# Three 256-column fp32r matmuls per weight tile into one accumulation, PSUM results read by their users, and a modulation reduced into rows, in a single-core two-block transformer kernel

## The reference, cut to what matters

```python
p  = rms_norm(x, norm_mix) @ w_in                       # w_in
h  = x + concat(rwkv7_group(p), dsa_group(p)) @ w_mix_out      # mixer, mix_out
h  = h + memory_cross_attention(rms_norm(h), rms_norm(mem))    # kv, q, o
h  = h + square(relu(rms_norm(h) @ w_up)) @ w_down      # mlp
h  = rms_norm(h, norm_final)                            # norm "final"
m  = silu(c) @ ada_w + ada_b                            # modulation: 6 vectors of 2048
n  = modulate(rmsnorm(h, g0), m[0], m[1])               # norm "g0"
z  = gelu(n @ a_w_in); u, v = split(z)                  # a_v, a_uo
s  = w_s . rmsnorm(v) + b_s                             # mixing over 128 tokens
h  = h + m[2] * ((u * s) @ a_w_out)                     # a_uo
n  = modulate(rmsnorm(h, g1), m[3], m[4])               # norm "g1"
g, v = split(dwconv(n @ ffn_w_up))                      # ffn, ffn_tail
h  = h + m[5] * ((silu(g) * v) @ ffn_w_down)
out = rmsnorm(h, final_g)                               # norm "out"
```

## Time and profile before

| | |
|---|---|
| time, median of 3 runs | 3272.32 us (3270.5 to 3272.33) |
| the profiled execution, its own time | 3279.74 us |
| its span in the profile | 3277.9 us |
| granted TensorE clock, mean | 0.924 |
| PE busy | 89% |
| PEld (weight loads) busy | 77% |
| DVE busy | 68% |
| ACT busy | 43% |
| HBM read | 568.08 MB, 174 GB/s over the span |
| chain that ended last | PE 82%, DVE 12%, issue 3%, ACT 2%, DMA 1% |

### The profile page before, as it was taken

The page is one execution under the profiler, slowest core; times in us unless marked ns, Lnnn a source line. Parts: engine busy times, 40 slices in busy tenths (PEclk is TensorE's granted clock), DMA queues, the critical chain, the costliest instruction groups (busy, mean ns, idle before and its releaser), DMA issues.

```text
span 3277.9 us, 49683 instructions
## 1 busy us (share of the span) xinstructions
PE 2922.4 (89%) x16638; PEld 2516.7 (77%) x16638; DVE 2228.9 (68%) x3447; ACT 1413.6 (43%) x2225; POOL 167.1 (5%) x204
## 2 busy tenths in 40 slices
PE   7997765665898899999999799799998999999997
PEld 6886654553686688888888678788887888888886
DVE  5445666656575887878878554588786775666666
ACT  5444121212444544444444255454444554554554
POOL 0002300000210100000001101000000000000001
PEclk9999777785798899999999699999998999999999
DMA  5553000010343577787877345277774555555553
GB/s 187 190 186 104 1 6 6 6 51 4 120 163 103 193 284 272 277 284 271 284 273 267 139 149 192 102 283 284 268 273 139 189 184 187 186 188 191 177 191 135
DMA packets 157042, 572.65 MB, mean 175 GB/s; under 512 B 17440, under 2 KB 17824, under 8 KB 156480
## 3 DMA queue, kind: packets, MB, share of 16 engines
q1 hardware_dynamic: 154512, 562.37, 49.8%
q10 hardware_dynamic: 2304, 7.75, 0.7%
q0 software_dynamic: 48, 0.13, 0.0%
HBM read 568.08 MB, written 2.10 MB: 174 GB/s over the span
## 4 chain that ended last, share of the span: by engine, by line
PE 82%; DVE 12%; issue 3%; ACT 2%; DMA 1%; DVEq 0%; POOL 0%; ACTq 0%; POOLq 0%; SPq 0%
PE ps L1684 45%; PE ps L1685 24%; PE ps L1687 3%; PE ps L1750 1%; DVE wlo L1403 1%; PE ps L598 1%; PE ps L587 1%; PE ps L604 1%; DVE xx L404 1%; ACT whi L1230 1%; DVE bt L385 1%; DVE lm L381 0%; PE ps L606 0%; DVE tt L1430 0%; DVE rn L357 0%
## 5 line engine op out<-in xcount | busy, mean ns | idle before, releaser
L1684 PE MATMUL ps<-xn,whi 128*128 128x512 f32 x4080 | 1457.3, 401 | 55.5 <-DVE xn L1469 36.0
L1403 DVE TENSOR_TENSOR wlo<-raw,whi 128x1024 fp32r<-128x1024 f32 x872 | 1058.5, 1228 | 445.7 <-ACT whi L1230 436.9
L1685 PE MATMUL ps<-xn,wlo 128*128 128x256 f32 x4352 | 1216.7, 282 | 0.0
L1230 ACT ACTIVATE whi<-raw 128x1024 fp32r<-128x1024 f32 x872 | 906.2, 1054 | 611.2 <-PE ps L1685 583.9
L1684 PEld LDWEIGHTS ps<-xn,whi 128*128 128x128 f32 x4080 | 773.5, 190 | 249.2 <-issue 48.1
L1684 PE MATMUL ps<-act_in,whi 128*128 128x512 f32 x2444 | 872.5, 401 | 11.2 <-issue 3.8
L1685 PEld LDWEIGHTS ps<-xn,wlo 128*128 128x128 f32 x4352 | 829.0, 190 | 5.6
L1685 PE MATMUL ps<-act_in,wlo 128*128 128x256 f32 x2624 | 732.3, 282 | 0.0
L1684 PEld LDWEIGHTS ps<-act_in,whi 128*128 128x128 f32 x2444 | 462.7, 189 | 126.9 <-DVE wlo L1403 5.2
L1685 PEld LDWEIGHTS ps<-act_in,wlo 128*128 128x128 f32 x2624 | 498.9, 190 | 3.9
L1237 ACT ACTIVATE hl<-ps 128x256 f32<-128x256 f32 x452 | 169.0, 376 | 388.6 <-PE ps L1687 388.6
(11 more groups left out here) (317 smaller groups left out, 2372.1 us busy)
## 6 DMA issues: line engine op xcount, KB each, us to landing
raw<-in_stream SPq DMA_DIRECT2D x872, 512.0 KB, 4.2
adaw<-in_ada SPq DMA_DIRECT2D x96, 512.0 KB, 5.9
adaq<-in_ada SPq DMA_DIRECT2D x96, 512.0 KB, 4.9
h<-in_xT SPq DMA_DIRECT2D x4, 512.0 KB, 6.7
lw<-in_lora ACTq DMA_DIRECT2D x8, 256.0 KB, 2.5
memx<-in_memT ACTq DMA_DIRECT2D x1, 2048.0 KB, 8.8
out<-fin SPq DMA_DIRECT2D x4, 512.0 KB, 2.6
wst<-in_wsT ACTq DMA_DIRECT2D x1, 1024.0 KB, 5.0
```

Source lines behind the costliest of these rows:

```text
L1230: act.activation(whi[:, r, :], raw[:, r, :], ACT.Copy).then_inc(hi_done, 1)
L1403: dve.tensor_tensor(wlo[:, r, :], raw[:, r, :], whi[:, r, :].bitcast(F32), ALU.subtract)\
L1684: pe.matmul(ps[:, b, :], whi[:, r, w], x[:, kc, :], start=first, stop=False)
L1685: ins = pe.matmul(ps[:, b, 0:T], wlo[:, r, w], x[:, kc, 0:T], start=False, stop=False)
```

## The change

- **Matmuls.** A pair becomes three matmuls of 256 columns, all into columns 0:256 of the bank: `whi` with the high part, `whi` with the low part, `wlo` with the high part. The order is the same in all chunks. There are 20928 stream matmuls in place of 13952, and as many weight loads; the columns are as many as before.
- **Evacuation.** `half`, `add`, `hl` and `evac_done` go. The user of a tile reads the bank: ACT copies (w_in, kv, q), relu (mlp), gelu (a_v, a_uo), copy and middle tap (ffn); DVE the residual add to `h`. Two counters, `evac_act` and `evac_dve`, say who has emptied a bank; `bank_free` makes PE wait for the right one. The mlp's square is a `tensor_tensor` on DVE.
- **Waits of the squares.** The wait for POOL's sums moves from DVE's residual to ACT's square.
- **Initial count.** `evac_act` is raised by 8 on ACT, behind `prepare("mix")`.
- **Tail.** For q, o, mlp, a_v and a_uo the four splits ahead stand behind the last tile in place of between the last tiles, on ACT and DVE.
- **Modulation.** PE multiplies each accumulator (512 columns, moving) with a 16- or 8-column slice of a mostly zero matrix `pick`, which puts the sum of accumulator a into row a of one bank; ACT copies the rows to SBUF (`rows`); four transposes turn them (`turn_modulation`). Part of this stands ahead of `stat` (5 of 16, 4 of 8), the rest behind it.

```diff
-def schedule(loop, iters, lens, split, evac, primed=False, ahead=None, aside=None):
+def schedule(loop, iters, lens, split, evac, primed=False, ahead=None, aside=None, tail_first=False):
...
                 split(i + 1, p - S)
-            elif ahead and p - S < RING:
+            elif ahead and p - S < RING and not tail_first:
                 ahead(0, p - S)
             for g, t in due.get(p, ()):
                 evac(i, g, t)
             if aside:
                 aside(i, p)
+        if last and ahead and tail_first:
+            for p in range(RING):
+                ahead(0, p)
...
+    def evacuated(self, i, g, t):
+
+        w = self.who[g]
+        return w, self.before[w] + 4 * (i * self.who.count(w) + self.who[:g].count(w)) + t + 1
...
+    EVAC = {"A": evac_act, "D": evac_dve}
+
+    def all_evacuated(eng, nm):
+
+        for w in "AD":
+            if L[nm].before[w]:
+                eng.wait_ge(EVAC[w], L[nm].before[w])
+
+    def bank_free(eng, lin, i, g, t):
+
+        if g >= 2:
+            w, v = lin.evacuated(i, g - 2, t)
+        elif isinstance(i, int) and i == 0 and lin.g0:
+            before, k, q = last_two[lin.g0 + g - 2]
+            w, v = before.evacuated(k, q, t)
+        else:
+            w, v = lin.evacuated(i - 1, len(lin.lens) + g - 2, t)
+        eng.wait_ge(EVAC[w], v)
 
...
-        def half(lin, i, g, t):
+        def copy_out(lin, i, g, t, dst):
 
             tile_wait(act, lin, i, g, t)
-            act.wait_ge(evac_done, lin.tile(i, g, t) + 5)
-            act.activation(hl[:, t, :], ps[:, lin.bank(g, t), T:2 * T], ACT.Copy).then_inc(hl_done, 1)
+            act.activation(dst, ps[:, lin.bank(g, t), 0:T], ACT.Copy).then_inc(evac_act, 1)
...
+                    act.wait_ge(EVAC[w], v)
+                    act.wait_ge(ss_done, SQ_AT[nm] + max(0, (2 if nm == "mlp" else 1) * (j - 3)))
                     act.activation(tt[:, t, :], h[:, j, :], ACT.Square).then_inc(sq_done, 1)
...
         prepare("mix")
-        run("w_in", half)
+        act.sem_inc(evac_act, 8)
+        run("w_in", lambda lin, i, g, t: copy_out(lin, i, g, t, one(proj[:, bass.ds(8 * i + 4 * g + t, 1), 1:TW])
+                                                  if not isinstance(i, int) else proj[:, 8 * i + 4 * g + t, 1:TW]))
         mixer["scalar"](act)
...
         def mlp(lin, i, g, t):
+            def relu(t):
+                tile_wait(act, lin, i, g, t)
+                act.wait_ge(ai_ready, AI["mlp"] + 16 * i + 4 * g + t + 1)
+                act.activation(tt[:, t, :], ps[:, lin.bank(g, t), 0:T], ACT.Relu).then_inc(evac_act, 1)
             if g < 4:
-                staged(t, lambda t: half(lin, i, g, t), lambda t: high("mlp", i, 4 * g + t))
+                staged(t, relu, lambda t: high("mlp", i, 4 * g + t))
             else:
-                staged(t, lambda t: half(lin, i, g, t), residual("mlp", i, 4)(g))
+                residual("mlp", i, 4)(g)(t)
         run("mlp", mlp)
+        def rows(nm, sums, n):
+
+            act.wait_ge(ada_red, 1 if nm == "g0" else 3)
+            act.activation(sums[0:n, 0, :], ps[0:n, red_bank[nm], :], ACT.Copy).then_inc(row_done, 1)
...
                 def middle(t):
 
-                    act.wait_ge(evac_done, lin.tile(i, g, t) + 9)
+                    tile_wait(act, lin, i, g, t)
+                    act.wait_ge(y_sum, 2 * (k4 + t) + 2)
+                    z = ps[:, lin.bank(g, t), 0:T]
+                    act.activation(zc[:, t, 1:T + 1], z, ACT.Copy).then_inc(z_done, 1)
+                    act.wait_ge(r_done, AI[nm] + 16 * i + 2 * g - 1 + t % 2)
                     apart(act)
                     a = FC[nm] + 16 * i + 2 * g + t % 2
                     c = COL["conv"] + 8 * a + 4 * (t // 2)
                     w = lambda q: par[:, c + q:c + q + 1] if isinstance(c, int) else par[:, bass.ds(c + q, 1)]
-                    act.activation(yc[:, t, :], zc[:, t, 1:T + 1], ACT.Identity, bias=w(3), scale=w(1))\
-                       .then_inc(y_done, 1)
+                    act.activation(yc[:, t, :], z, ACT.Identity, bias=w(3), scale=w(1)).then_inc(evac_act, 1)
...
+                    tile_wait(dve, L[nm], i, g, t)
+                    y = ps[:, L[nm].bank(g, t), 0:T]
+                    if gate is None:
+                        ins = dve.tensor_tensor(h[:, m, :], y, h[:, m, :], ALU.add)
                     else:
-                        dve.wait_ge(ss_done, SQ_AT[nm] + max(0, m - 3))
-                    add(L[nm], i, g, t, tt[:, t, :])
-                    dve.wait_ge(evac_done, L[nm].tile(i, g, t) + 9)
-                    if gate is None:
-                        ins = dve.tensor_tensor(h[:, m, :], h[:, m, :], tt[:, t, :], ALU.add)
-                    else:
-                        ins = dve.scalar_tensor_tensor(h[:, m, :], tt[:, t, :], mod[:, gate + m:gate + m + 1],
+                        ins = dve.scalar_tensor_tensor(h[:, m, :], y, mod[:, gate + m:gate + m + 1],
                                                        h[:, m, :], ALU.mult, ALU.add)
-                    ins.then_inc(h_sum, 1)
+                    ins.then_inc(evac_dve, 1)
...
                         if first:
-                            pe.wait_ge(evac_done, lin.tile(i, g, t) + 1)
-                        b = lin.bank(g, t)
+                            bank_free(pe, lin, i, g, t)
+                        y = ps[:, lin.bank(g, t), 0:T]
                         w = slice(c * 512 + t * P, c * 512 + (t + 1) * P)
-                        if not last:
-                            pe.matmul(ps[:, b, :], whi[:, r, w], x[:, kc, :], start=first, stop=False)
-                        ins = pe.matmul(ps[:, b, 0:T], wlo[:, r, w], x[:, kc, 0:T], start=False, stop=False)
-                        if last:
-                            ins = pe.matmul(ps[:, b, :], whi[:, r, w], x[:, kc, :], start=False, stop=True)
-                            if t < 3:
-                                ins.then_inc(tile_done, 1)
+                        pe.matmul(y, whi[:, r, w], x[:, kc, 0:T], start=first, stop=False)
+                        pe.matmul(y, whi[:, r, w], x[:, kc, T:2 * T], start=False, stop=False)
+                        ins = pe.matmul(y, wlo[:, r, w], x[:, kc, 0:T], start=False, stop=last)
+                        if last and t < 3:
+                            ins.then_inc(tile_done, 1)
                 ins.then_inc(slot_used, 1)
...
+        def reduce_modulation(nm, after, sums, n, part):
+
+            b = red_bank[nm]
+            bank_free(pe, L[after], 0, 0, 1)
+            for a in part:
+                pe.wait_ge(ada_sum, 7 + 2 * ((0 if nm == "g0" else ADA_MLP) + 8 * a + 8))
+                ins = pe.matmul(ps[0:n, b, :], pick[:, 15 - a:15 - a + n], sums[:, a, :], start=a == 0, stop=a == n - 1)
+            if n - 1 in part:
+                ins.then_inc(ada_red, 1)
+
+        def turn_modulation(nm, sums, n):
+
+            pe.wait_ge(row_done, 1 if nm == "g0" else 2)
+            for t in range(4):
+                ins = pe.transpose(ps[:, red_bank[nm], t * n:(t + 1) * n], sums[0:n, 0, t * P:(t + 1) * P], ident[0:n, 0:n])
             ins.then_inc(ada_red, 1)
-        reduce_modulation("g0", L["a_v"].g0, ada, 16)
-        stat("final", L["a_v"].g0)
+        reduce_modulation("g0", "a_v", ada, 16, range(5))
+        stat("final", first_free("a_v"))
         pe.matmul(ps[:, stat_bank["final"], T:2 * T], ones[:, :], sg[:, :], start=True, stop=True).then_inc(stat_done, 1)
+        reduce_modulation("g0", "a_v", ada, 16, range(5, 16))
```

More of the change, by code:

```diff
@@ L885, in one @@
         return x.rearrange("p a c -> p (a c)")
-    L, n, g = {}, 0, 0
-    for name, it, lens in [("w_in", 6, [8, 8]), ("mix_out", 1, [8] * 4), ("kv", 1, [8, 8]), ("q", 1, [8]),
-                           ("o", 1, [2] * 4), ("mlp", 4, [8] * 8), ("a_v", 4, [8, 8]), ("a_uo", 2, [8] * 8),
-                           ("ffn", 2, [8] * 12), ("ffn_tail", 1, [8] * 6 + [6] * 4)]:
-        L[name] = Lin(n, g, lens, it)
+    L, n, g, before, last_two = {}, 0, 0, {"A": 8, "D": 0}, {}
+    for name, it, lens, who in [("w_in", 6, [8, 8], "AA"), ("mix_out", 1, [8] * 4, "DDDD"), ("kv", 1, [8, 8], "AA"),
+                                ("q", 1, [8], "A"), ("o", 1, [2] * 4, "DDDD"), ("mlp", 4, [8] * 8, "AAAADDDD"),
+                                ("a_v", 4, [8, 8], "AA"), ("a_uo", 2, [8] * 8, "AAAADDDD"),
+                                ("ffn", 2, [8] * 12, "AAAAAAAADDDD"), ("ffn_tail", 1, [8] * 6 + [6] * 4, "AAAAAADDDD")]:
+        L[name] = Lin(n, g, lens, it, who, dict(before))
         n += it * sum(lens)
         g += it * len(lens)
+        for w in "AD":
+            before[w] += 4 * it * who.count(w)
+        for q in range(len(lens)):
+            last_two[g - len(lens) + q] = (L[name], it - 1, q)
     NSLOT = n
@@ L901, in build @@
              "ffn": "ffn_tail"}
+    TAIL_FIRST = ("q", "o", "mlp", "a_v", "a_uo")
     w_landed = [sem(f"w_landed{r}") for r in range(RING)]
@@ L926, in build @@
```

(21 more changed lines are left out.)

165 lines of the change are left out of this document (79 added, 86 removed).

## The result

The changed kernel takes 3303.07 us (median of 4, 3301.97 to 3304.11) against 3272.32; ratio 1.0094, interval 1.0077 to 1.0112. Its profiled execution took 3303.39, with a span of 3301.6. I had forecast 3241 and a range up to 3266.

What follows compares the result with a forecast made beforehand. PE was taken as the bound, its 6976 pairs filling some 2460 of 3278 us. Terms summing to -30.8 took the profiled 3279.74 to 3248.9; less 7.4, that execution's excess over the median, 3241, range 3221 to 3266.

Steps and rivals of the forecast that it cites:

- The stream: PE's matmul stream: three 256-column matmuls take 0.3532 us where a pair took 0.353, +3 us (bounds -15 to +19).
- Rival 1: PE's matmul stream: a third weight load shows, 16 ns each, +112 us, 3353 us; chance 0.09.
- Rival 2: Longer loop bodies of w_in and a_v pay 1.6 to 2.9 us a turn, +15 us, 3256 us; chance 0.07.
- The start: First matmul of w_in waits for ACT's increment behind prepare("mix"), not before 41.4 instead of 30.34: +10.7 us.
- The first modulation: From mlp's end to the first modulation: norm "final" starts earlier and the reduction gets shorter, -24 us (-27.3 to -17.4).
- The second: From a_uo to the second modulation: eight matmuls, four hidden ahead of stat, replace 64 records, -12.3 us (-12.8 to -11.2).
- o to mlp: PE's 1.60 us loss to a late wlo inside o goes and the mlp norm starts earlier: -4.8 us.
- q: From q to cross-attention: DVE must finish four splits ahead of its copy of vx, +1.2 us.
- a_v: From a_v to mixing: stat comes some 3 us earlier, but the fourth split ends at 2081.8, +0.3 us.
- Small waits: At w_in's end, norms of mem and cross, kv's tail, mlp's last turn, ffn_tail's end: shorter way out, -4.9 us.

## Why the prediction was wrong

**The stream**, +3 by my sum, +49 measured. This step decided it: with the stream at +3 and all else as measured, the kernel would have taken some 3257 (3303 - 46), inside the range; with all else as forecast and the stream at +49, 3287, outside it. The step that failed is the price of 256 columns, "0.115 to 0.118 for 256 columns whatever stands ahead". I had taken it from 256-column matmuls that stand beside 512-column ones. The reading was right as far as it went: the 113 cases of two in a row at full clock, all at group ends, are 0.118 apart. But in the stream the two widths together cost 353, and how the trace shares it (236 and 117) says nothing of what either costs alone: 512 among its like takes 227 and 256 takes 120. I also took the mixer's 0.108 to 0.113 for a load with its matmul as proof that the load leaves room at 0.118. It is the floor of narrow matmuls and holds; but above it the price is columns and some 13 ns, not the greater of the two. My upper bound, 0.3555 a trio, left no place for 0.3600. A bound "from both sides" for a form that the trace never shows in a row should have reached to rival 1's.

**Rival 1** had the mechanism, a price for each matmul that 512 columns pay once, and named 4.8 ns a pair as the point from which it decides; 7.0 came. Its size was wrong, 16 ns for half of an overhead of 33, so its time was 3353. I gave it 0.09 because I asked only whether a load fits behind a matmul. The Trainium skill, "Perfetto Trace Analysis", Identifying the Most-Contended Engine, which takes the weight loads' busy share as the measure, pointed the right way: the share rose from 77% to 87%. It doesn't give the size, since 0.19 us loads start 0.12 apart here too.

**Rival 2**, longer code, also came true, and not where I had put it. w_in and a_v, with 384 matmuls a turn, show no gap at all. The mlp and a_uo (1536 a turn, 1024 before) and ffn (2304 for 1536), whose gaps I had held for paid, grew: 1.6 to 2.9 us became 3.8 to 4.9, and ffn's 0.9 became 2.6. The error was to take a cost that exists already as fixed, when the thing that it scales with grew by half. And I had not seen what follows: behind a pause of some 4 us the granted clock is 0.50, behind one of 1.6 to 2 it is not (behind those of 2.3 to 3.1 in all runs it is in some cases), and that is nearly as dear again, 9 us. The Trainium skill, "Runtime: NRT & Kernel Launch", Instruction fetch mechanics, has a taken branch outside the window wait for a fetch; the traces agree in that only the long bodies pay, that a 16 KB packet of the instruction queue starts 2.6 to 3.7 us ahead of PE's going on at each turn, and that writing the loops out ends the pause. The pause is this time less the lead of the packet over PE's last matmul: before, the packet started 0.4 to 1.5 us ahead of that matmul at the turns of mlp and a_uo, after the change 1.0 to 2.1 behind it. Bodies of 1408 and 1344 matmuls, in the run with nine widths, lie between (pauses of 3.2 to 3.9). Length alone doesn't give the pause: ffn's body is the longest and its pause the shortest, and its packet starts earliest (1.8 ahead before, 0.2 ahead after). What sets the packet's start no run here tells.

**The start**: +10.7 forecast (41.4 less 30.34 is 11.1; the sum was off by 0.4), +9.2 measured, and 7.5 by moving one line. **The first modulation**: -24 forecast, -24.4 measured. The path is as described, and the size is right in part by luck. The norm came 11.8 us behind the last stream matmul, not 10.7, straight behind DVE's fourth split; but PE's `stat` ended within 0.1 us of that split and not 1.5 earlier, 2.5 us later than forecast. The 11 matmuls behind it took 10.57 us, 0.96 each, and not 12.0: the first 1.5 of them fell at clock 0.50, where I had put 3, and the rest took 0.86. The hop from the last of them to the modulation took 1.2 for 2.3. **The second**: -12.3 and -12.9. **o to mlp**: -4.8 and -4.2 (PE's stall of 2 us inside o, is gone; the norm starts 7.6 behind PE's last instead of 9.8). DVE there:

```profile
1088.90 1.50 DVE L1545 TENSOR_TENSOR h<-ps,h 128x256 f32<-128x256 f32 x4 [4.01 <-PE ps L1719]
1091.83 5.51 DVE L1460 TENSOR_TENSOR wlo<-raw,whi 128x1024 fp32r<-128x1024 f32 x4 [1.43 <-ACT whi L1265]
1097.26 0.41 DVE L1504 TENSOR_SCALAR hl<-ps 128x256 f32<-128x256 f32 x1
```

**q**: +1.2 forecast; `vx` is copied 6.2 us behind the last matmul of q instead of 5.4, +0.9, and from there to o's first matmul more than half of it is won back. **a_v**: +0.3 forecast, -0.5 measured. **Small waits**: -4.9 forecast, about -6.5; the wait at the norm of mem fell from 3.23 to 1.52, and with it the slow stretch behind it. All that isn't the stream or a turn came to some -44 (23.7 less 68) against my -33.8; the parts named here give some -38, and I put the rest down to slow stretches that no longer follow a shorter pause, which I did not add up one by one.

So the sum of the parts on the queues was good to a few microseconds each, and the two terms on the bottleneck engine itself, which I had set at +3 and 0, came to 68.

## What to carry to other kernels

Where PE is the bound, count matmuls and not only columns: in this kernel one over 224 columns costs its columns and some 13 ns, and a pitch taken from a mixed sequence is no price for either of its parts. Replacing 512 columns by twice 256 to spare two other engines work that is hidden behind PE buys nothing where it is spent most. Look at what an engine's loop already pays at its turn before you make the body longer, and at the granted clock behind the pause; and look for what stands ahead of an initial `sem_inc` on its own engine.

## What the runs showed of the hardware

- At full clock, load and matmul start 111 to 112 ns apart for 128, 192 and 224 columns, and above that columns / 2.4 GHz and 12 to 14 ns (20 at 448).
- 512 and 256 columns by turns cost either 353 ns a pair, 6 more than each among its like, or 347, no more. One or the other holds for tens to hundreds of microseconds. Before the change nearly all was at 353, with the old stream in the new kernel more than half at 347. Four of a width in a row cost 351.
- At clock 0.50 the price for each is gone: three times 256 and 512 with 256 both take 0.64 a tile and chunk, the bare columns at 1.2 GHz.
- The turn of PE's loop over mlp or a_uo costs 3.8 to 5.0 us where the body has 1536 matmuls, with 3.4 to 6.8 us granted at 0.50 behind or across its end; 3.2 to 3.9 where it has 1344 or 1408; 1.0 to 3.3 where it has 1024; nothing in w_in and a_v with 384. The longest body, ffn's, costs less: 0.9 to 1.5 with 1536, 2.6 to 3.1 with 2304.
- At each of these turns PE goes on 2.6 to 3.7 us behind the start of a 16 KB packet of the instruction queue; in the loop of w_in (110 to 300 in the changed kernel) no such packet comes.
- 22 records (11 matmuls) of 512 fp32 columns with 16 columns of weights took 10.57 us, 0.86 a matmul at full clock; the 64 with one moving column and a whole load of weights each had kept DVE idle for 28.61, at clock 0.50.
